# A third buffer for the modulation tiles, and six halves in the strip ring in place of eight

## The reference

```python
sh1, sc1, g1, sh2, sc2, g2 = split(silu(c) @ w_mod + b_mod, 6)      # w_mod: 2048 x 12288
hm = rms_norm(x) * (1.0 + sc1) + sh1
q, k, v, o, g = split(hm @ w_in)                                    # w_in: 2048 x 6160
x = x + g1 * (mlstm(q, k, v, o, g) @ w_out)                         # 8 heads, w_out: 2048 x 2048
hf = rms_norm(x) * (1.0 + sc2) + sh2
u = causal_conv3(hf @ w_up) + conv_b                                # w_up: 2048 x 11264
x = x + g2 * ((silu(u[gate]) * u[val]) @ w_down)                    # w_down: 5632 x 2048
```

## Time and profile before

| | us |
|---|---|
| median of 3 runs | 1202.1 |
| the profiled execution's own time | 1202.58 |
| its span | 1200.8 |
| TensorE matmul busy | 1170.5 (97%) |
| VectorE busy | 916.9 (76%) |
| ScalarE busy | 627.2 (52%) |
| mean granted TensorE clock | 0.982 of full speed |

### The profile page before, as it was taken

One profiled execution on the slowest core, in us unless ns is written; L12 is line 12 of the kernel. 1 busy time (PEld: TensorE's weight loads), 2 busy tenths in 40 slices (PEclk: granted clock), 3 DMA queues, 4 the chain that ended last, 5 costly groups with the idle time before them and its releaser, 6 DMA issues.

```text
span 1200.8 us, 17196 instructions
## 1 busy us (share of the span) xinstructions
PE 1170.5 (97%) x5922; PEld 999.4 (83%) x5922; DVE 916.9 (76%) x992; ACT 627.2 (52%) x912; POOL 147.7 (12%) x152
## 2 busy tenths in 40 slices
PE   5799999999999999999999999999999999999998
PEld 5788888878888888888888888888888888888887
DVE  5799978789988998988887446888885446777654
ACT  4354565655654456565554445555554545555442
POOL 0000020100012210222121000212211000221100
PEclk9599999999999998999999999999999999999999
DMA  9999989899999993898885568879865566766542
GB/s 361 359 386 401 399 292 388 304 376 344 347 359 355 389 317 115 242 268 230 231 244 204 184 207 244 233 212 259 235 212 208 180 203 178 195 188 183 202 166 80
DMA packets 260441, 314.56 MB, mean 262 GB/s; under 512 B 6208, under 2 KB 186888, under 8 KB 251688
## 3 DMA queue, kind: packets, MB, share of 16 engines
q1 hardware_dynamic: 259360, 312.51, 78.4%
q0 software_dynamic: 592, 1.22, 0.4%
q10 hardware_dynamic: 442, 0.21, 0.1%
HBM read 311.80 MB, written 2.11 MB: 261 GB/s over the span
## 4 chain that ended last, share of the span: by engine, by line
PE 86%; DMA 8%; DVE 3%; issue 1%; SPq 1%; ACT 0%; POOL 0%; DVEq 0%; ACTq 0%
PE ps L1231 27%; PE ps L1237 14%; PE ps L1271 9%; PE ps L1273 9%; PE ps L1272 9%; DMA m<-in_l_w_mod_dram 7%; PE ps L1318 4%; PE ps L1320 4%; PE ps L1319 4%; DVE acc L967 1%; DMA mod_raw<-in_l_w_mod_dram 1%; PE ps L1341 1%; SPq L342 1%; DVE acc L940 1%; PE ps L1346 1%
## 5 line engine op out<-in xcount | busy, mean ns | idle before, releaser
L927 DVE TENSOR_TENSOR w_lo<-raw,w_hi 128x1024 fp32r<-128x1024 f32 x392 | 482.2, 1231 | 185.8 <-ACT w_hi L567 183.8
L567 ACT ACTIVATE w_hi<-raw 128x1024 fp32r<-128x1024 f32 x392 | 414.0, 1057 | 351.0 <-PE ps L1273 167.9
L1231 PE MATMUL ps<-hm,w_hi 128*128 128x512 f32 x1408 | 340.2, 392 | 1.7 <-DVE hm L1159 1.7
L1231 PEld LDWEIGHTS ps<-hm,w_hi 128*128 128x128 f32 x1408 | 258.3, 189 | 50.8 <-issue 1.9
L1237 PEld LDWEIGHTS ps<-hm,w_lo 128*128 128x128 f32 x1408 | 183.2, 192 | 8.6 <-DVE w_lo L927 0.2
L1237 PE MATMUL ps<-hm,w_lo 128*128 128x256 f32 x1408 | 185.5, 283 | 0.0
L1318 PE MATMUL ps<-w_hi,hm 128*128 128x512 f32 x384 | 156.4, 407 | 3.2 <-DVE hm L978 2.7
L1320 PE MATMUL ps<-w_hi,hm 128*128 128x512 f32 x384 | 151.8, 395 | 0.0
L1319 PE MATMUL ps<-w_lo,hm 128*128 128x512 f32 x384 | 151.7, 395 | 0.0
L1271 PE MATMUL ps<-w_hi,act_hi 128*128 128x512 f32 x344 | 134.2, 390 | 0.0
L1273 PE MATMUL ps<-w_hi,act_lo 128*128 128x512 f32 x344 | 133.8, 389 | 0.0
(11 more groups left out here) (169 smaller groups left out, 1064.2 us busy)
## 6 DMA issues: line engine op xcount, KB each, us to landing
raw<-in_l_w_up_dram SPq DMA_DIRECT2D x88, 1024.0 KB, 5.9
mod_raw<-in_l_w_mod_dram SPq DMA_DIRECT2D x56, 1024.0 KB, 6.4
raw<-in_l_w_in_dram SPq DMA_DIRECT2D x96, 512.0 KB, 8.1
raw<-in_l_w_down_dram SPq DMA_DIRECT2D x44, 1024.0 KB, 5.0
m<-in_l_w_mod_dram SPq DMA_DIRECT2D x32, 640.0 KB, 7.2
raw<-in_l_w_out_dram SPq DMA_DIRECT2D x16, 1024.0 KB, 8.5
m<-in_l_w_mod_dram SPq DMA_DIRECT2D x16, 768.0 KB, 13.7
mod_wide<-in_l_w_mod_dram SPq DMA_DIRECT2D x8, 1024.0 KB, 7.0
```

Of the source, the lines that this page charges most:

```text
L567: nc.scalar.activation(w_hi[:, v % 4, :], raw[:, v // 2 % 4, (v % 2) * HALF:(v % 2 + 1) * HALF], ACT.Copy).then_inc(w_hi_made, 1)
L927: nc.vector.tensor_tensor(w_lo[:, v % 4, :], raw[:, v // 2 % 4, (v % 2) * HALF:(v % 2 + 1) * HALF], w_hi[:, v % 4, :].bitcast(f32), ALU.su ...
L1231: return mm(ps[:, 4 + w % 4, :], w_hi[:, v % 4, j * P:(j + 1) * P], both, start=(k == 0), stop=stop, skip_group_check=True)
```

## The change

The strip ring has six halves in place of eight while the input projection runs, and the 8 KB per partition of the last two become a third buffer, `mod_third`, for the modulation tiles 0 to 31, which then go round three buffers. From the output projection on the ring has its four units again; its fourth unit waits for the modulation tiles that used the place. A half waits for the half six before it, a tile for the tile three before it. The places of the tiles in the queue (`MOD_LOAD`) follow: three at the start, then 10 slots behind the add that frees them. In pass 0 the queue is four halves in place of six, and then m1 tile i followed by half 4+i. The numbers of loads, splits, adds and matmuls are the same.

```diff
--- before.py
+++ after.py
@@ -72,8 +72,12 @@
 
     MOD_WIDE = 2 * KT
     WIDE_LOADS = KT // 4
-
-    MOD_LOAD = [V_PASS1 + 5, V_PASS1 + 6] + [max(V_PASS1 + 6, p + 11) for p in MOD_SLOT[:MOD_WIDE]] \
+    RAW_HALVES, MOD_BUFS = 6, 3
+    MOD_USES = (MOD_WIDE + MOD_BUFS - 1) // MOD_BUFS
+
+    MOD_LOAD = [V_PASS1 + 5 + k for k in range(MOD_BUFS)] \
+        + [max(V_PASS1 + 5 + MOD_BUFS, p + 10) for p in MOD_SLOT[:MOD_WIDE - MOD_BUFS]] \
+        + [p + 11 for p in MOD_SLOT[MOD_WIDE - 2:MOD_WIDE]] \
         + [V_OUT + 11, V_OUT + 11] + [max(V_OUT + 11, p + 11) for p in MOD_SLOT[MOD_WIDE:-4]]
 
 
@@ -95,6 +99,7 @@
 
 
         raw = place("raw", [P, 4, UNIT], 0)
+        mod_third = place("mod_third", [P, UNIT], 24 * KB)
         mod_raw = place("mod_raw", [P, 2, UNIT], 32 * KB)
         m0 = place("m0", [P, 8, 2 * M0_COLS], 0)
         m1 = place("m1", [P, 3, M1_COLS], 32 * KB)
@@ -196,7 +201,7 @@
         w_hi_made = sem("w_hi_made")
         half_done = sem("half_done")
         evac0, seeded, evac1 = sem("evac0"), sem("seeded"), sem("evac1")
-        mod_in = [sem(f"mod_in{s}") for s in range(2)]
+        mod_in = [sem(f"mod_in{s}") for s in range(MOD_BUFS)]
         wide_in = [sem(f"wide_in{s}") for s in range(2)]
         mod_done = sem("mod_done")
         acc_cleared = sem("acc_cleared")
@@ -263,8 +268,13 @@
                 j = k - MOD_WIDE
                 if j % 4 >= 2:
                     return mod_wide[:, j % 2, :], wide_in[j % 2], j // 4 + 1
-                return mod_raw[:, j % 2, :], mod_in[j % 2], MOD_WIDE // 2 + j // 4 + 1
-            return mod_raw[:, k % 2, :], mod_in[k % 2], k // 2 + 1 - (WIDE_LOADS if k >= 3 * KT else 0)
+                return mod_raw[:, j % 2, :], mod_in[j % 2], MOD_USES + j // 4 + 1
+            s = k % MOD_BUFS
+            return mod_raw[:, s, :] if s < 2 else mod_third[:], mod_in[s], k // MOD_BUFS + 1
+
+        def raw_half(v):
+            s = v % RAW_HALVES if v < V_OUT else v % 8
+            return raw[:, s // 2, (s % 2) * HALF:(s % 2 + 1) * HALF]
 
         def strip_of(vh):
 
@@ -313,7 +323,12 @@
         def _(sp):
             def load(use, src, shape_k, plus=0):
 
-                sp.wait_ge(raw_done, plus * 2 + 2 * use + 2)
+                if use < U_OUT + RAW_HALVES // 2:
+                    sp.wait_ge(raw_done, RAW0 + V_OUT - RAW_HALVES + 2 * (use - U_OUT) + 2)
+                else:
+                    if use == U_OUT + RAW_HALVES // 2:
+                        sp.wait_ge(mod_done, 2 + MOD_WIDE)
+                    sp.wait_ge(raw_done, plus * 2 + 2 * use + 2)
                 sp.sem_inc(sp_began, 1)
                 dst = raw[:, use % 4, :].rearrange("p (k n) -> p k n", k=shape_k)
                 sp.dma_start(dst, src).then_inc(raw_in[use % 4], 16)
@@ -325,8 +340,10 @@
                     sp.wait_ge(half_done, V_OUT)
                 elif MOD_WIDE + 4 <= k < 3 * KT:
                     sp.wait_ge(mod_done, k - 1)
-                else:
-                    sp.wait_ge(mod_done, plus + k + 1)
+                elif k >= MOD_WIDE:
+                    sp.wait_ge(mod_done, k + 1)
+                elif k >= MOD_BUFS:
+                    sp.wait_ge(mod_done, 2 + k - MOD_BUFS + 1)
                 sp.sem_inc(sp_began, 1)
                 sp.dma_start(dst, w_mod[mod_rows(tile), col:col + D]).then_inc(landed, 16)
 
@@ -357,11 +374,11 @@
                 n, m, kp = strip_of(vh)
                 kind, j = PASS[n][m - n * STRIPS]
                 col = STRIP_COL[kind] + QUARTER * j
-                if vh < 8:
-                    wait_m0((8, 9, 9, 10, 11, 11, 12, 13)[vh])
+                if vh < RAW_HALVES:
+                    wait_m0((8, 9, 9, 10, 11, 11)[vh])
                 else:
-                    sp.wait_ge(raw_done, vh + 1)
-                sp.dma_start(raw[:, vh // 2 % 4, (vh % 2) * HALF:(vh % 2 + 1) * HALF]
+                    sp.wait_ge(raw_done, RAW0 + vh - RAW_HALVES + 1)
+                sp.dma_start(raw_half(vh)
                              .rearrange("p (k n) -> p k n", k=2),
                              w_in[2 * kp * P:2 * (kp + 1) * P, col:col + QUARTER]
                              .rearrange("(k p) n -> p k n", p=P)).then_inc(half_in[vh % 8], 16)
@@ -383,12 +400,12 @@
                 sp.dma_start(x[:, t, :], x_d[0, t * P:(t + 1) * P, :]).then_inc(x_in[t], 16)
             for i in range(16):
                 load_m0(i)
-            for vh in range(6):
+            for vh in range(4):
                 load_half(vh)
             for i in range(2 * KT):
                 load_m1(i)
-                load_half(6 + i)
-            for vh in range(6 + 2 * KT, V_OUT):
+                load_half(4 + i)
+            for vh in range(4 + 2 * KT, V_OUT):
                 load_due_mods(vh)
                 load_half(vh)
 
@@ -564,9 +581,7 @@
                 elif v % 2 == 0:
 
                     act.wait_ge(raw_in[v // 2 % 4], 16 * ((v - V_OUT) // 8 + 1) + 2 * plus)
-                nc.scalar.activation(w_hi[:, v % 4, :],
-                                     raw[:, v // 2 % 4, (v % 2) * HALF:(v % 2 + 1) * HALF],
-                                     ACT.Copy).then_inc(w_hi_made, 1)
+                nc.scalar.activation(w_hi[:, v % 4, :], raw_half(v), ACT.Copy).then_inc(w_hi_made, 1)
 
             def slot_hi(p):
 
@@ -924,8 +939,7 @@
                 if v >= 2 * N_UNITS:
                     return
                 dve.wait_ge(w_hi_made, v + 1 + plus)
-                nc.vector.tensor_tensor(w_lo[:, v % 4, :],
-                                        raw[:, v // 2 % 4, (v % 2) * HALF:(v % 2 + 1) * HALF],
+                nc.vector.tensor_tensor(w_lo[:, v % 4, :], raw_half(v),
                                         w_hi[:, v % 4, :].bitcast(f32), ALU.subtract)\
                          .then_inc(raw_done, 1)
 
@@ -1172,7 +1186,7 @@
 
             def add_g2(tile, plus):
                 dve.wait_ge(acc_ready[1], 16 * 2)
-                dve.wait_ge(mod_in[0], 16 * (MOD_WIDE // 2 + WIDE_LOADS + tile + 1) + 16 * plus)
+                dve.wait_ge(mod_in[0], 16 * (MOD_USES + WIDE_LOADS + tile + 1) + 16 * plus)
                 dve.wait_ge(mod_done, 2 + 3 * KT + tile + plus)
                 nc.vector.scalar_tensor_tensor(out=acc[:, 1, :], in0=mod_raw[:, 0, :],
                                                scalar=cT[:, ds(tile + plus, 1)], in1=acc[:, 1, :],
```

## The result

The changed kernel takes 1210.5 us, the median of 4 runs (1210.03 to 1211.94), against 1202.2 for the kernel before (also a median of 4): 0.7% slower, ratio 1.0071 with a 95% interval of 1.0055 to 1.0087. The forecast was 1208.0 us, slower at 68%, range 1199.5 to 1217.0. Its profiled execution took 1210.66 us at a span of 1208.9, 8.1 us more than before.

What follows compares the result with a forecast made beforehand. Transfers were taken to bound the kernel up to 150 us, TensorE later. Profiled 1202.58 us, +10.1 for the first pass, -4.2 for the third buffer, 0.5 lower for the median: 1208.0 us, range 1199.5 to 1217.0.

Steps and rivals of the forecast that it cites:

- What bounds the first pass: Up to 150 us: transfers; the three-slot loop grows from 8.8 to 9.65 us, now through the half, its split and low part.
- Its size: First pass: the last m1 add ends at 158.78 us against 148.68, +10.1 us, bounds +4.9 and +19.9.
- the start: First pass: slots 1 to 3 fed from the queue's backlog, VectorE's part in slot 2 beginning at 59.56 us.
- the pair's latency: First pass, from the tile's issue to the half's landing: 5.8 us taken, between 5.28 and 6.78, plus 3.85 of other steps.
- The cover of the queue: First pass: half 6+i lay in the ring two slots before use; without this cover, even the byte floor costs +3.6 us.
- Rival 1: First pass: no bubble in the queue, only the byte floor holds, +3.6 - 4.2, 1201.5 us, not slower; 20%.
- The clock behind the last add: After the first pass: TensorE's wait might bring a longer stretch at 1.2 GHz; taken at nothing, bounds -1.6 to +1.6 us.
- Six halves: After the first pass: six halves in place of eight stay hidden, cost 0, bounds 0 to +2 us.
- The third buffer: Modulation stage after 150 us: waits of tiles 12 and 13, the gated tile's wait and slow clock go, -4.2 us.
- Rival 2: Modulation stage: the third buffer returns nothing and the gated tile stays late, +10.1, 1212.2 us; 12%.
- Rivals 3 and 4: First pass: pairs take 6.78 us each, 1217.8 us, 8%; or it costs under 2 us, 1199.9 or less, 5%.

Runs made afterwards that it cites:

- e2: The kernel before (ring of eight, two modulation buffers) with only four halves first, then m1 tile i and half 4+i: 1215.4 us, ratio 1.0108.
- e3: The changed kernel with five halves first, then m1 tile i and half 5+i: 1199.0 us, ratio 0.9973 to the kernel before.
- e4: The changed kernel with half 4+i issued ahead of m1 tile i, the same queue as e3: 1199.0 us, ratio 0.9975 to the kernel before.
- e1: The changed kernel with the first pass's queue as before, six halves first, then m1 tile i and half 6+i: 1197.1 us, ratio 0.9956 to the kernel before.
- e5: The changed kernel with three halves first, then m1 tile i and half 3+i: 1253.2 us, ratio 1.0424, 42.7 us over the changed kernel.
- e6: The changed kernel with two modulation buffers and six halves ahead as in e1, ring of six kept: 1201.8 us, ratio 0.9997 to the kernel before.

## Why the prediction was right

- **What bounds the first pass, and that the loop would change: right.** The chain of the changed kernel runs through the half. From slot 2 to slot 32 VectorE's part moves from 58.15 to 157.62 us: 9.95 us for three slots, where 9.65 was taken. e2 shows the step alone (+13.3 us), e3 and e4 (one queue, tried twice) that it is gone with one place more.
- **Its size was a little small.** The forecast had +10.1 us for the last add, measured +11.6. Of the start, 1.4 us went the other way: the first add starts at 56.55 us here, at 57.94 before, and at 56.97 to 57.57 in e1, e3 and e4. It does not follow the number of halves ahead (57.56 in e2 with four, 57.01 in e5 with three), and why it differs stays open. The loop itself costs 13.0 us from first add to last (102.2 against 89.2 us). The term was mis-sized in the pair's latency and what comes with it: 6.1 us in place of 5.8 is what 9.95 - 3.85 leaves. That is 3.0 us over ten rounds, of which the earlier start hid half; in part the near hit of the term is luck.
- **The cover of the queue: right.** Rival 1 (the bytes bind, only 3.6 us; once called the second rival in the prediction) fell: the rate was 351 to 365 GB/s and not 400. The estimate by the fit of the Trainium skill ("DMA: Bandwidth & Descriptors", Anatomy of one DMA), 4.7 us for the pair, would have led there; the section gives that fit for one transfer issued from GpSimd, and these are two, issued by SyncE. The trace does not agree: a pair issued at 144.16 us in the changed kernel took 0.39 + 5.0 us at a rate below 370 GB/s.
- **The clock behind the last add: taken at nothing within -1.6 to +1.6 us; measured +1.0.** TensorE's longer wait put the column sums at 1.2 GHz.
- **Six halves: right,** nothing (e6, 0.9997 with an interval that holds 1).
- **The third buffer: right in each step.** The waits of tiles 12 and 13 went, the wait for the gated head and its slow clock with them; -4.3 us by the trace, -4.7 and -4.9 by the times of e6 against e1 and of e2 against the changed kernel, where -4.2 was forecast. Rival 2 fell. The 1.6 us of slow clock in it are the less certain part (see e6).
- **Rivals 3 and 4 fell** with the latency: 6.78 us was met for a few pairs, not as the rule of the stage, and the first pass did not come near costing under 2 us.

## What to carry to other kernels

When a prefetch moves back in a queue, count the slots to its use and the steps that stand between its landing and the event that frees the next buffer: here the half had two more steps (split, low part) than the tile beside it, and the loop closed through it as soon as its use fell into the slot of the add. Look also at which wait of the issuing engine a load stands behind: here one place more of lead, which is the same as putting the half ahead of its tile and of the tile's wait, was worth 11.5 us of the 13.4. And a lead in a queue need not be constant: deep where the queue would run empty, shallow ahead of the transfer on which the next stage waits.

## What was not expected of the hardware

The column sums, ten matmuls with one column each, took 2.29 us behind a wait of 5.29 us and 1.27 us behind one of 0.96 us, with the granted clock at 0.50 from 160 to 162 us in the first case. A wait is no sure sign of the lower clock: behind one of 0.96 us it fell in the kernel before (0.50 from 152 to 154 us), and behind one of 2.58 us in e6 it did not. And the slower loop did shorten the queue, but on the whole not to the empty one's 5.28 us: from 97 to 151 us, with pairs 3.3 us apart in the mean, a pair took 5.2 to 7.2 us from the tile's issue to the half's landing, 6.0 in the mean, at a DMA share of 0.97 to 0.99.
